# Expert matrices read eight rows to a partition, and every eighth column in the gather and the turns

## The reference

```python
def expert_choice_ffn(xn, w_router, w_gate, w_up, w_down):
    B, S, D = xn.shape
    cap = CAPACITY_FACTOR * S // N_EXPERTS          # 64 tokens an expert, 16 experts
    aff = jax.nn.softmax(jnp.einsum('bsd,de->bse', xn, w_router).astype(jnp.float32), axis=-1)
    top_aff, top_idx = lax.top_k(jnp.swapaxes(aff, 1, 2), cap)
    bidx = jnp.arange(B)[:, None, None]
    xg = xn[bidx, top_idx]
    hid = jax.nn.silu(jnp.einsum('becd,edf->becf', xg, w_gate)) * jnp.einsum('becd,edf->becf', xg, w_up)
    y = jnp.einsum('becf,efd->becd', hid, w_down) * top_aff[..., None].astype(xn.dtype)
    return jnp.zeros((B, S, D), dtype=y.dtype).at[bidx, top_idx].add(y)
```

## Time and profile before

| what | us |
|---|---|
| median of 3 runs | 2144.54 (2142.96 to 2146.76) |
| the profiled execution, whole | 2142.04 |
| its span, first to last instruction | 2140.3 |
| PE busy | 1983.9 (93%) |
| PEld busy | 1441.6 (67%) |
| POOL busy | 1018.2 (48%) |
| DVE busy | 797.5 (37%) |
| ACT busy | 532.3 (25%) |

### The profile page before, as it was taken

One profiled execution on the slowest core, in us unless ns is written; L12 is line 12 of the kernel. 1 busy time (PEld: TensorE's weight loads), 2 busy tenths in 40 slices (PEclk: granted clock), 3 DMA queues, 4 the chain that ended last, 5 costly groups with the idle time before them and its releaser, 6 DMA issues.

```text
span 2140.3 us, 23254 instructions
## 1 busy us (share of the span) xinstructions
PE 1983.9 (93%) x9424; PEld 1441.6 (67%) x9424; DVE 797.5 (37%) x1186; ACT 532.3 (25%) x1119; POOL 1018.2 (48%) x580
## 2 busy tenths in 40 slices
PE   8998897978999999998999999989979999999977
PEld 6777786757777888886866668867854444443436
DVE  2544558453213401333454375553230111111135
ACT  4534436322322200112033342332210000000032
POOL 5786657736556877886634486446500000000015
PEclk9999998999999999999999999999979999999998
DMA  5321112312222333322311122212759999999971
GB/s 179 89 69 30 40 60 79 128 40 89 69 69 70 99 99 91 97 97 79 121 53 55 50 79 79 60 50 70 276 198 409 409 409 409 409 409 409 409 279 59
DMA packets 117882, 335.74 MB, mean 157 GB/s; under 512 B 8689, under 2 KB 10353, under 8 KB 117521
## 3 DMA queue, kind: packets, MB, share of 16 engines
q1 hardware_dynamic: 113296, 321.55, 41.8%
q10 hardware_dynamic: 4336, 12.19, 1.6%
q0 software_dynamic: 144, 0.52, 0.1%
HBM read 327.95 MB, written 6.29 MB: 156 GB/s over the span
## 4 chain that ended last, share of the span: by engine, by line
PE 80%; DVE 7%; DMA 5%; POOL 4%; ACT 3%; issue 2%; PEldq 0%; DVEq 0%; ACTq 0%; PEld 0%; SPq 0%; POOLq 0%
PE bank L540 48%; PE bank L1691 12%; PE bank L1721 3%; PE bank L1708 2%; PE bank L702 2%; DMA shared<-in_w_exp_gate 2%; PE bank L441 1%; POOL shared_r L565 1%; POOL shared_r L564 1%; PE bank L1363 1%; DMA arena<-in_w_exp_up 1%; PE bank L1376 1%; DMA arena<-in_w_exp_gate 1%; DMA shared<-in_w_exp_down 1%; DVE arena L1625 1%
## 5 line engine op out<-in xcount | busy, mean ns | idle before, releaser
L540 PE MATMUL bank<-shared_r 128*128 128x512 f32 (+1 forms) x4032 | 952.5, 392 | 19.2 <-POOL shared_r L565 9.5
L540 PEld LDWEIGHTS bank<-shared_r 128*128 128x128 f32 x4032 | 739.5, 192 | 191.0 <-issue 25.9
L564 POOL TENSOR_TENSOR shared_r<-shared,small 128x1024 fp32r<-128x1024 f32 (+1 forms) x184 | 355.3, 1931 | 986.3 <-DMA shared<-in_w_ple_gate 530.7
L565 POOL TENSOR_TENSOR shared_r<-shared,shared_r 128x1024 fp32r<-128x1024 f32 (+1 forms) x184 | 456.1, 2479 | 14.4
L632 DVE TENSOR_TENSOR X<-bank,X 128x512 f32<-128x512 f32 x96 | 66.4, 692 | 427.9 <-PE bank L1708 240.8
L1691 PE MATMUL bank<-shared,arena 128*64 128x512 f32 x864 | 191.3, 594 | 10.5 <-DMA shared<-in_w_exp_gate 4.0
L540 PE MATMUL bank<-shared_r,arena_r 128*128 128x512 f32 x768 | 176.1, 391 | 0.0
L540 PEld LDWEIGHTS bank<-shared_r,arena_r 128*128 128x128 f32 x768 | 144.2, 188 | 31.5
L1691 PE MATMUL bank<-arena 128*64 128x512 f32 x672 | 149.3, 594 | 6.7 <-DMA arena<-in_w_exp_gate 1.9
L1691 PEld LDWEIGHTS bank<-shared,arena 128*64 128x64 f32 x864 | 67.4, 137 | 129.6 <-issue 119.8
L583 POOL TENSOR_TENSOR shared_r<-shared,shared_r 128x1024 fp32r<-128x1024 f32 x32 | 80.3, 2509 | 82.3 <-ACT shared_r L574 82.3
(11 more groups left out here) (383 smaller groups left out, 2027.8 us busy)
## 6 DMA issues: line engine op xcount, KB each, us to landing
shared<-in_w_in SPq DMA_DIRECT2D x80, 512.0 KB, 3.6
shared<-in_w_exp_up SPq DMA_DIRECT2D x38, 1024.0 KB, 18.3
shared<-in_w_exp_down SPq DMA_DIRECT2D x36, 1024.0 KB, 18.5
shared<-in_w_exp_gate SPq DMA_DIRECT2D x34, 1024.0 KB, 18.4
arena<-in_w_exp_gate SPq DMA_DIRECT2D x30, 1024.0 KB, 18.5
arena<-in_w_exp_down SPq DMA_DIRECT2D x28, 1024.0 KB, 18.4
arena<-in_w_exp_up SPq DMA_DIRECT2D x26, 1024.0 KB, 18.1
shared<-in_w_up SPq DMA_DIRECT2D x32, 512.0 KB, 3.7
```

What stands on the lines that cost most here:

```text
L540: ins = pe.matmul(dst, W_, x_, start=first, stop=final)
L564: link(pool.tensor_tensor(hi, raw(p), small[:, 18:19].to_broadcast([P, hi.shape[1]]), ALU.add))
L565: pool.tensor_tensor(lo, raw(p), hi.bitcast(F32), ALU.subtract).then_inc(S_("w_split"), 1)
```

## The change

A partition now holds eight consecutive rows of each expert matrix: row 8 p + 2 c + r lies in partition p, chunk c, place r. The chunk's two rows are neighbours, so a partition's share of a panel is one run of 8192 bytes, and the runs of neighbouring partitions begin 32 KiB apart. Group k is then made of the rows k, k + 8, k + 16, ... To match, the gather and the turns take every eighth column (`d::KT`, `q::KT`, with KT = 8): 128 elements 32 bytes apart. The gain is laid out in the same order (eight more columns that the host writes, read at `PT[:, 1, 32:40]`). As the first group of turned columns now spans both halves of the hidden rows, PE waits for both halves before the first turn. The ring, the counts, the matmuls and their order stay.

```diff
     def expert_load(sp, q):
 
         e, c, w, i = q % 2, q // 2 % 4, q // 8 % 3, q // 24
-        src = A[("w_exp_gate_2", "w_exp_up_2", "w_exp_down_2")[w]][0, 2 * i + e, 2 * c * P:(2 * c + 2) * P, :]
+        src = A[("w_exp_gate_2", "w_exp_up_2", "w_exp_down_2")[w]][0, 2 * i + e].rearrange("(p c r) n -> c p (r n)", c=4, r=2)[c]
         if q >= RING:
             sp.wait_ge(S_("x_used"), (q - RING) // 2 + 1)
-        sp.dma_start(ring[q % RING].rearrange("p (k n) -> p k n", k=2), src.rearrange("(k p) n -> p k n", p=P)).then_inc(panels_full[q // 2 % (RING // 2)], 16)
+        sp.dma_start(ring[q % RING], src).then_inc(panels_full[q // 2 % (RING // 2)], 16)
...
                 for j in range(ST):
-                    ins = pe.matmul(bank[:, dd * P:(dd + 1) * P], XS[:, j, d * P:(d + 1) * P], OH[i % 2][:, j].rearrange("p e c -> p (e c)"),
+                    ins = pe.matmul(bank[:, dd * P:(dd + 1) * P], XS[:, j, d::KT], OH[i % 2][:, j].rearrange("p e c -> p (e c)"),
                                     start=j == 0, stop=j == ST - 1)
...
+        pe.wait_ge(S_("hid"), 2 * i + 2)
         for h in range(2):
             n = x_bank["t", i, h]
             bank = bank_claim(pe, n)
-            pe.wait_ge(S_("hid"), 2 * i + h + 1)
             for kk in range(4):
                 q = 4 * h + kk
-                ins = pe.transpose(bank[:, kk * P:(kk + 1) * P], HG[:, q * P:(q + 1) * P], ident[:, :])
+                ins = pe.transpose(bank[:, kk * P:(kk + 1) * P], HG[:, q::KT], ident[:, :])
             bank_ready(ins, n)
...
-        which, c0 = COL["norm_ffn_2"]
+        which, c0 = 1, 32
...
+    cols[:, 1, 32:40] = arrays["in_norm_ffn_2"].reshape(P, KT)
```

## The result

| what | before, us | after, us |
|---|---|---|
| median of 6 runs each | 2144.01 (2141.64 to 2146.76) | 2192.13 (2189.10 to 2193.90) |
| the profiled execution's span | 2140.3 | 2190.2 |

The ratio is 1.0222, 95% interval 1.0209 to 1.0236: the changed kernel is 48 us slower, where 12 us faster was forecast. It is the first rival, at about half speed.

What follows compares the result with a forecast made beforehand. Expert transfers at 409 GB/s were taken to set PE's pace once the ring drained. The terms -12.5 + 0.66 - 0.6 = -12.4 us gave 2129.6, or 2132 as median; own range 2127 to 2139, 8-in-10 range 2124 to 2164.

Steps and rivals of the forecast that it cites:

- the first rival: Strided load slower, PE becomes the bound: 2189 us at half speed, 2160 at 160 ns a load; chance 0.21.
- Part 1: Expert panel transfers in runs of 8192 bytes instead of 4096: 421 GB/s instead of 409, gain 12.5 us.
- the 9 ns per packet: DMA transfers: doubling the run costs 75.5 ns, not 84.7, so about 9 ns per packet are not bytes.
- the line through two run lengths: DMA packet times, 84.7 ns at 2048 bytes and 160.2 at 4096, extended to 311.2 ns at 8192, or 421 GB/s.
- Part 2: Gather and turns reading every eighth column: taken to cost 0, between 0 and a load at half speed (57 us).
- the row of a strided read: DVE reads 32 elements 516 bytes apart in 173 ns, 4 contiguous in 180; taken to show PE's step costs nothing.
- the upper end: PE's strided load at half speed, taken from the router at clock 0.50: 99 ns more a load, 57 us.
- Part 3: Merged wait for both halves before the turns: covered in seven pairs, +0.66 us once in the last.
- Part 4: Behind the experts, DVE's 4-element sum L418 is blocked for less time by a POOL pass: -0.6 us.
- Rivals 2 and 3: 2: run length gives nothing, 409 GB/s stays, 2145 us, chance 0.12; 3: 32 KiB pitch costs rate, 2170, chance 0.05.
- rival 4: Half the way: 5 to 15 ns more a load, or 415 GB/s: -4.5 to -9 us; chance 0.07.

Runs made afterwards that it cites:

- loads_only: The changed kernel's transfers, with gather and turns reading columns side by side as before; other numbers come out of the experts: 2132.21 us, ratio 0.9941.
- dealt_xs: The changed kernel with normalised tokens written already sorted by DVE and ACT, so the gather reads side by side: 2130.68 us, ratio 0.9933.
- turns_step8: The changed kernel with only the gather put back to columns side by side; the turns keep every eighth column: 2129.35 us, ratio 0.9933.
- rows2_dealt: The changed kernel with two rows per partition instead of eight, tokens written already sorted, and one wait per half: 2129.50 us, ratio 0.9938.
- rows2: The changed kernel with two neighbouring rows per partition instead of eight (step 8 bytes) and one wait per half: 2129.82 us, ratio 0.9934.
- gather_step3: The changed kernel with the gather reading every third column (12 bytes) and the turns contiguous: 2157.90 us, one run (before 2138.58).
- rows4: The changed kernel with four neighbouring rows per partition instead of eight (step 16 bytes) and one wait per half: 2186.41 us, ratio 1.0205.

## Why the prediction was wrong

**Part 1, right.** 421 GB/s was forecast and 421 measured, with no price for the pitch; gathers "58.9 us apart to the end" is what loads_only shows. Its span is 13.5 us shorter than before; the forecast of parts 1, 3 and 4 was 12.4 (span 2127.9, measured 2126.8). What the 9 ns per packet beside its bytes are is not known; the line through two run lengths was enough.

**Part 2, the step that failed.** "Between the ends I go by the row of a strided read ... I take 0." The ends were right, the choice between them was not: +127 ns a load in the gather (242.5 - 115), beyond even the upper end of 99. Two things were wrong with the row taken. It has 32 elements; in dealt_xs DVE pays 1.20 us / 6 = 200 ns for 512 strided elements, 0.39 ns each, which would be 12 ns on 32 elements and can't be read off an operation of 173 ns, beside another kind of operation that needs 180 for 4 elements. And it is of another engine: at 32 bytes PE pays 1.0 ns more per element (127 / 128) where DVE pays 0.39. The argument that a load with one column in 0.87 ns "asks for addresses no faster than DVE at 0.96 GHz does by much" looked at the rate of addresses; what counts is lines. The part had the right frame, though: 111 of the gather's 115 ns are the load, so nothing hid it.

The upper end fell short because it took the load of before at half the clock (200 to 211 ns). The strided load isn't that load made slower. The first gather shows it: at a granted clock of 0.50 (the 1.2 GHz level) its loads start as far apart as at the full clock, 4.3 us / 18 = 239 ns and 8.4 us / 35 = 240 ns. The loads of the two stretches, count and first and last start:

```profile
L1721 PEld LDWEIGHTS bank<-arena x19: 313/338/341, 1585.9 to 1590.2; 128*128 128x128 f32 x19
...
L1721 PEld LDWEIGHTS bank<-arena x36: 334/337/338, 1592.1 to 1600.5; 128*128 128x128 f32 x36
```

Timeline of PE, after:

```profile
1585.86 15.62 PE L1721 MATMUL bank<-arena 128*128 128x128 f32 x64 [1.04 <-DVE arena L1770]
```

and before:

```profile
1583.81 9.98 PE L1721 MATMUL bank<-arena 128*128 128x128 f32 x64 [1.04 <-DVE arena L1770]
```

Before, the first gather lost 2.6 us to the clock; after, 0.1. So it costs +5.6 and not +8.1, and the granted clock doesn't set its pace.

The count failed the other way: 576 loads were to pay, 512 do. The turns' loads got 47 ns longer and cost nothing (turns_step8). Eight strided turn loads in 0.96 us, each 188 ns long, are (0.96 - 0.19) / 7 = 110 ns apart, less than half of what the gather's need for as many lines. Their load was shorter to begin with (141 against 192 ns); why, and why the step costs them less, no run shows. In sum 512 x 0.127 = 65 us, less the 2.5 us of the first gather, is the +62.6 of the balance, where 0 was taken and 57 was the bound. That the bound came so near is luck: the price per load was too low and the number of loads too high.

**Part 3, right in kind**: in loads_only the down product starts at 2037.80, the figure worked out. Of the +0.66 about 0.5 is seen: from the last gather to the down product loads_only needs 61.05 us, and rows2_dealt, with a wait for each half, 60.58. **Part 4, right in sign**: L418 1.38 us in loads_only, 1.0 less than before (0.6 forecast). In after it isn't a matter of 1 us: the last scatter starts 6.5 us behind POOL's first pass where it started 2.3 us ahead of it, and the whole stall goes.

**The rivals.** The first had the mechanism and the threshold: 22 ns a load, and rows2 with 6.6 ns gained, gather_step3 with 63 lost. It said 2189 at half speed; 2192 came, with the two errors above against each other. Its signs were a gather of 10 to 14 us and turns of 1.3 to 2; 15.52 and 1.04 came. Its chance of 0.12 (0.21 in all) was too small: one row of another engine, at a size where the effect can't be seen, should not have outweighed a gather with no cover whatever and the rule that the prediction itself cites against it. Rivals 2 and 3 are refuted by loads_only, rival 4 by the 127 ns a load. The spread was taken too small as well: the three runs of before reach 0.10% from their median and not 0.09%, and the 13 runs beside the later kernels 0.34%.

## What to carry to other kernels

Where a layout is bought with a step on chip, count the 16-byte lines an operand touches and who hides them: in this gather two fp32 elements per line are nearly free (+6.6 ns a load), one per line doubles the time of a 128-column fp32 matmul, and a gather made of such loads has nothing to hide it. The turns don't follow this count, so measure each kind of read. Long runs for the transfers don't need a large step: two neighbouring rows per partition gave the same 8192-byte runs and the same 421 GB/s as eight. When a price is taken from an analogous row, check first that the row is long enough for the effect to be seen in it.

## What the runs showed of the hardware

- PE reading fp32 with a step in the gather, full clock: 115 ns per 128 elements side by side, 121.6 at 8 bytes, 178.4 at 12, 237 at 16, 242.5 at 32, 222 at 64; 237 at 32 bytes when the operand is the streamed one. That 64 bytes is cheaper than 16 was not expected and isn't explained.
- The turns at 32 bytes run at the old pace (8 in 1.04 us), but at 8 bytes (rows2, rows2_dealt) and at 16 (rows4) 8 take 1.12 us, with loads of 209 ns where 32 bytes has 188. So lines don't order the turns; this isn't explained either.
- The strided read hardly depends on PE's clock or on the transfers beside it: the first gather, partly at 0.50 and with the DMA idle, takes 15.62 us and the others 15.52, where before it was 9.98 and 7.38 us.
- A DVE sum of 4 elements that starts during a POOL pass of 128 x 1024 ends with the pass (2.35 us in rows2_dealt, 1.38 in loads_only), and takes 0.16 us with no pass beside it.
- DVE on 512 fp32 elements 32 bytes apart: +200 ns an operation; ACT 1.18 us against 0.67 (pairs: 2.36 against 1.33); at 8 bytes apart (rows2_dealt) six DVE operations take 2.47 us against 2.46, and ACT's pair 1.44.
- DMA at saturation: 387, 409 and 421 GB/s in runs of 2048, 4096 and 8192 bytes, runs of neighbouring partitions 32 KiB apart in the last.
